# x also given with its columns on partitions: the opening loads, multiplies and waits of an encoder block rearranged

## What is computed

```python
n = rms_norm(h, norm1_g[l])
p = n @ w_in[l]                       # (256 x 1024) @ (1024 x 1536)
qa, ka, va, qb, kb, vb = jnp.split(p, splits, axis=-1)
...
ob = mixer_window(qb, kb, vb, sink[l], rel_bias)   # scores + rel_bias[bucket], then softmax
mix = jnp.concatenate([rms_norm(oa, gnorm_a[l]), rms_norm(ob, gnorm_b[l])], axis=-1)
h = h + mix @ w_o[l]
h = h + hier_moe(rms_norm(h, norm2_g[l]), w_group[l], b_group[l], w_expert[l], b_expert[l],
                 w_gate[l], w_up[l], w_down[l])
```

## Time and profile before

| | us |
|---|---|
| median of 3 runs | 605.11 (604.78 to 606.01) |
| the profiled execution | 604.16 |
| its span in the profile | 602.3 |
| PE busy | 514.4 (85% of the span) |
| DVE, ACT, POOL busy | 132.3, 71.0, 28.2 |
| moved by DMA | 217.56 MB, mean 361 GB/s |

### The profile page before, as it was taken

The page is one execution under the profiler, slowest core; times in us unless marked ns, Lnnn a source line. Parts: engine busy times, 40 slices in busy tenths (PEclk is TensorE's granted clock), DMA queues, the critical chain, the costliest instruction groups (busy, mean ns, idle before and its releaser), DMA issues.

```text
span 602.3 us, 6699 instructions
## 1 busy us (share of the span) xinstructions
PE 514.4 (85%) x2681; PEld 240.9 (40%) x2681; DVE 132.3 (22%) x308; ACT 71.0 (12%) x140; POOL 28.2 (5%) x58
## 2 busy tenths in 40 slices
PE   4999799978999999999999999999959553855294
PEld 2445577546444453535353535353514110411031
DVE  1005565334102020303030303030303000300023
ACT  2013324131010101010101000000100000000002
POOL 2032020040000000000000000000000000000001
PEclk9999999986999999999999999999989856986699
DMA  6898491152889999999999999999999999999991
GB/s 251 326 385 365 175 383 13 36 207 108 299 344 432 425 423 430 429 428 429 430 428 429 427 429 430 429 428 427 425 431 427 428 424 431 429 425 429 414 373 72
DMA packets 23944, 217.56 MB, mean 361 GB/s; under 512 B 5041, under 2 KB 6089, under 8 KB 12401
## 3 DMA queue, kind: packets, MB, share of 16 engines
q1 hardware_dynamic: 19680, 214.31, 85.3%
q10 hardware_dynamic: 4240, 2.94, 1.6%
HBM read 216.18 MB, written 1.06 MB: 361 GB/s over the span
## 4 chain that ended last, share of the span: by engine, by line
PE 71%; DMA 22%; SPq 3%; DVE 2%; issue 1%; ACT 0%; POOL 0%; DVEq 0%; POOLq 0%; ACTq 0%
PE bank L1206 27%; PE bank L1221 13%; PE bank L1178 7%; DMA ring<-in_w_down_dram 7%; PE bank L1241 6%; DMA ring<-in_w_gate_dram 5%; DMA ring<-in_w_up_dram 5%; PE bank L1073 5%; PE bank L1004 4%; DMA ring<-bias_line 3%; PE bank L1063 2%; SPq L366 2%; PE bank L1041 1%; PE bank L1052 1%; PE bank L987 1%
## 5 line engine op out<-in xcount | busy, mean ns | idle before, releaser
L1206 PE MATMUL bank<-ring,region_x 128*64 128x512 f32 (+1 forms) x1024 | 191.9, 636 | 50.6 <-DMA ring<-in_w_up_dram 27.6
L1206 PEld LDWEIGHTS bank<-ring,region_x 128*64 128x64 f32 (+1 forms) x1024 | 60.8, 134 | 178.7 <-issue 178.7
L1221 PE MATMUL bank<-ring,region_q 128*64 128x512 f32 (+1 forms) x512 | 95.7, 624 | 7.0 <-DMA ring<-in_w_down_dram 5.7
L874 DVE TENSOR_TENSOR region_q<-region_q,bank 128x512 f32<-128x512 f32 x13 | 8.9, 687 | 312.5 <-PE bank L1206 312.5
L1221 PEld LDWEIGHTS bank<-ring,region_q 128*64 128x64 f32 (+1 forms) x512 | 29.7, 131 | 63.8 <-issue 61.4
L1178 PE MATMUL bank<-region_q,region_t 128*128 128x128 f32 x416 | 51.1, 284 | 1.8 <-DVE region_q L861 1.8
L1241 PE MATMUL bank<-region_x,region_q 128*128 128x512 f32 x104 | 50.6, 618 | 0.7 <-ACT region_x L606 0.7
L1178 PEld LDWEIGHTS bank<-region_q,region_t 128*128 128x128 f32 x416 | 50.1, 200 | 1.8 <-issue 1.8
L1004 PE MATMUL bank<-ring,region_x 128*128 128x512 f32 x96 | 42.6, 596 | 2.2 <-DMA ring<-in_w_in_dram 1.4
L880 DVE TENSOR_TENSOR h<-h,bank 128x512 f32<-128x512 f32 x52 | 35.7, 687 | 21.9 <-PE bank L1241 21.9
L606 ACT ACTIVATE region_x<-bank 128x512 f32<-128x512 f32 x26 | 15.5, 597 | 135.0 <-PE bank L1221 135.0
(11 more groups left out here) (172 smaller groups left out, 248.5 us busy)
## 6 DMA issues: line engine op xcount, KB each, us to landing
ring<-in_w_gate_dram SPq DMA_DIRECT2D x32, 2048.0 KB, 18.4
ring<-in_w_up_dram SPq DMA_DIRECT2D x31, 2048.0 KB, 16.1
ring<-in_w_down_dram SPq DMA_DIRECT2D x27, 2048.0 KB, 18.1
ring<-in_w_down_dram SPq DMA_DIRECT2D x20, 512.0 KB, 13.8
ring<-in_w_in_dram SPq DMA_DIRECT2D x8, 768.0 KB, 9.4
ring<-in_w_o_dram SPq DMA_DIRECT2D x2, 2048.0 KB, 8.6
ring<-in_w_up_dram SPq DMA_DIRECT2D x4, 512.0 KB, 5.6
ring<-bias_line ACTq DMA_DIRECT2D x1, 1536.0 KB, 15.4
```

Of the source, the lines that this page charges most:

```text
L874: dve.tensor_tensor(act_sb, silu_sb, ps[UP][:], ALU.mult).then_inc(act_done, 1)
L1206: last = pe.matmul(ps[bank][rows, :], xgT[:, c, rows], slots[fill_slot(f + a)][:, c * F:(c + 1) * F], start=(c == 0), stop=(c == KC - 1))
L1221: last = pe.matmul(ps[GD0 + half][rows, :], hT[:, c, rows], slots[fill_slot(f + a)][:, c * D + 512 * half:c * D + 512 * half + 512], start ...
```

## The change

The host hands over two more tensors: `x_cols`, x with its columns on partitions (1 MB, in the layout of `xT`), and `gain_cols`, the norm weights in the layout of `gT`. The rows of x are loaded too, for the squares' sums and the residual.

- SP loads `gT`, then `xT` in four pieces (256 KB each) alternating with the first four chunks of `w_in`; after the sixth chunk come the rows of x, then the last two chunks, then `cst`. Only then does SP wait, for `bias_in`, ahead of `w_o` and the first experts. The waits inside `w_in` are gone.
- The transposes of the norm weights and of x on PE are gone, and their copies on DVE. DVE multiplies `xT` in place, one chunk of 128 x 256 at a time.
- PE waits for each chunk of `xT` by itself.
- DVE sets 128 x 640 numbers to zero, and PE multiplies zeros with zeros: two products with 512 columns ahead of line 979's product, and two behind it. Nothing reads their results.
- ACT issues the bias load ahead of the squares' sums, and only when the sixth chunk of `w_in` has landed.
- PE's wait for `cst` moves from ahead of the first transpose to ahead of the first transpose of the attention.

```diff
--- before.py
+++ after.py
@@ -196,6 +195,7 @@
+        zeros = region_t[:, 0:640]
...
@@ -297,19 +298,16 @@
 
         @block.sync
         def _(sp):
+            sp.dma_start(gT[:], gain_cols).then_inc(gain_in, 16)
+            for c in range(KC):
+                if c < 4:
+                    sp.dma_start(xT[:, 2 * c:2 * c + 2, :], x_cols[:, 2 * c:2 * c + 2, :]).then_inc(xT_in[c], 16)
+                sp.dma_start(w_in_sb[:, c, :], w_in_c[c]).then_inc(w_in_in[c], 16)
+                if c == 5:
+                    for t, arrived in enumerate((x_in, x1_in)):
+                        sp.dma_start(h[:, t, :], x_t[t]).then_inc(arrived, 16)
             sp.dma_start(cst[:], consts).then_inc(consts_in, 16)
-            for t, arrived in enumerate((x_in, x1_in)):
-                sp.dma_start(h[:, t, :], x_t[t]).then_inc(arrived, 16)
-            sp.dma_start(gain_rows[0:8, :], norm1_g.rearrange("l (c p) -> (l c) p", p=P)).then_inc(gain_in, 16)
-            sp.dma_start(gain_rows[8:12, :], gnorm_a.rearrange("l (c p) -> (l c) p", p=P)).then_inc(gain_in, 16)
-            sp.dma_start(gain_rows[12:16, :], gnorm_b.rearrange("l (c p) -> (l c) p", p=P)).then_inc(gain_in, 16)
-            sp.dma_start(gain_rows[16:24, :], norm2_g.rearrange("l (c p) -> (l c) p", p=P)).then_inc(gain_in, 16)
-            for c in range(KC):
-                if c == 3:
-                    sp.wait_ge(line_stored, 16)
-                if c == 7:
-                    sp.wait_ge(bias_in, 16)
-                sp.dma_start(w_in_sb[:, c, :], w_in_c[c]).then_inc(w_in_in[c], 16)
+            sp.wait_ge(bias_in, 16)
             sp.dma_start(w_o_sb[:, 4:8, :], w_o_c[:, 4:8, :]).then_inc(slot_in[4], 16)
...
@@ -476,17 +473,17 @@
 
             act.wait_ge(line_ready, 1)
             act.activation(line_sb, ps[7][0:8, :], ACT.Copy).then_inc(line_cut, 1)
-            act.wait_ge(x_in, 16)
-            act.activation(junk, h[:, 0, :], ACT.Square, accum_out=ssx[:, 0:1]).then_inc(ssx_ready, 1)
             act.wait_ge(line_masked, 1)
             act.dma_start(bias_line, line_sb).then_inc(line_stored, 16)
-            act.wait_ge(x1_in, 16)
-            act.wait_ge(ssx_ready, 1)
-            act.activation(junk, h[:, 1, :], ACT.Square, accum_out=ssx[:, 1:2]).then_inc(ssx_ready, 1)
             act.wait_ge(line_stored, 16)
+            act.wait_ge(w_in_in[5], 16)
             shifted = bass.AP(bias_line.tensor, 0, [[1, P], [4 * P, 8], [1, 3 * P]])
             act.dma_start(bias_sb, shifted).then_inc(bias_in, 16)
-
+            for t, arrived in enumerate((x_in, x1_in)):
+                act.wait_ge(arrived, 16)
+                if t:
+                    act.wait_ge(ssx_ready, 1)
+                act.activation(junk, h[:, t, :], ACT.Square, accum_out=ssx[:, t:t + 1]).then_inc(ssx_ready, 1)
 
             act.wait_ge(rstd1_ready, 1)
@@ -639,14 +636,12 @@
                 ins.then_inc(dve_chain, 1)
                 dve.wait_ge(dve_chain, n[0])
 
-            dve.wait_ge(gains_turned, 1)
-            link(dve.tensor_copy(gT[:], ps[6][:, 0:24]))
-            for t in range(TT):
-                for b in range(2):
-                    dve.wait_ge(x_turned, 2 * t + b + 1)
-                    dve.tensor_tensor(xT[:, 4 * b:4 * b + 4, t * P:(t + 1) * P],
-                                      ps[(4 if t == 0 else 6) + b][:].rearrange("p (c t) -> p c t", c=4),
-                                      bcast(gT[:, 4 * b:4 * b + 4], 2, P), ALU.mult).then_inc(xT_ready, 1)
+            dve.memset(zeros, 0.0).then_inc(zeros_ready, 1)
+            dve.wait_ge(gain_in, 16)
+            for c in range(KC):
+                if c % 2 == 0:
+                    dve.wait_ge(xT_in[c // 2], 16)
+                dve.tensor_scalar(xT[:, c, :], xT[:, c, :], gT[:, c:c + 1], None, ALU.mult).then_inc(xT_ready, 1)
 
             dve.wait_ge(k_squared, 1)
@@ -975,26 +970,21 @@
 
         @block.tensor
         def _(pe):
+            def multiply_zeros(n):
+                for _ in range(n):
+                    pe.matmul(ps[6][:], zeros[:, 0:P], zeros[:, P:P + 512], start=True, stop=True)
+
+            pe.wait_ge(zeros_ready, 1)
+            multiply_zeros(2)
             pe.wait_ge(onehot_in, 32)
             pe.matmul(ps[7][0:8, :], relb_sb, onehot_sb, start=True, stop=True).then_inc(line_ready, 1)
-            pe.wait_ge(consts_in, 16)
-            pe.wait_ge(gain_in, 16 * 4)
-            pe.transpose(ps[6][:, 0:24], gain_rows[0:24, :], ident[0:24, 0:24]).then_inc(gains_turned, 1)
+            multiply_zeros(2)
 
             def turn(dst, srcs, done):
 
                 for k, src in enumerate(srcs):
                     last = pe.transpose(dst[:, k * P:k * P + src.shape[0]], src, ident[0:src.shape[0], 0:src.shape[0]])
                 last.then_inc(done, 1)
-
-            pe.wait_ge(x_in, 16)
-            for b in range(2):
-                turn(ps[4 + b], [h[:, 0, c * P:(c + 1) * P] for c in range(4 * b, 4 * b + 4)], x_turned)
-            pe.wait_ge(x1_in, 16)
-            pe.wait_ge(line_cut, 1)
-            pe.wait_ge(xT_ready, 1)
-            for b in range(2):
-                turn(ps[6 + b], [h[:, 1, c * P:(c + 1) * P] for c in range(4 * b, 4 * b + 4)], x_turned)
...
@@ -1004,8 +994,8 @@
                 return pe.matmul(ps[bank][:], xT[:, c, t * P:(t + 1) * P], cols, start=(c == 0), stop=(c == KC - 1))
 
 
-            pe.wait_ge(xT_ready, 4)
             for c in range(KC):
+                pe.wait_ge(xT_ready, c + 1)
                 pe.wait_ge(w_in_in[c], 16)
                 qkv(0, KV, c, 0)
                 qkv(1, KV, c, 1)
@@ -1076,6 +1066,7 @@
                 return last
 
 
+            pe.wait_ge(consts_in, 16)
             pe.wait_ge(qkv_cut, 3)
             turn(ps[4], [pair_cols(0, b) for b in range(5, 9)], qk_turned)
@@ -1343,7 +1334,10 @@
     nc = _bacc.Bacc("TRN2", target_bir_lowering=False, num_devices=1)
     arrays, args = {}, []
     consts, onehot = shape_constants()
-    every = [(n, inputs[n]) for n in _INS] + [("consts", consts), ("onehot", onehot)]
+    x_cols = inputs["x"][0].reshape(S, KC, P).transpose(2, 1, 0)
+    gain_cols = _np.concatenate([inputs[n][0].reshape(-1, P).T for n in ("norm1_g", "gnorm_a", "gnorm_b", "norm2_g")], 1)
+    every = [("x", inputs["x"]), ("x_cols", x_cols), ("gain_cols", gain_cols)]
+    every += [(n, inputs[n]) for n in _INS[1:]] + [("consts", consts), ("onehot", onehot)]
```

9 lines of the change are left out of this document (4 added, 5 removed).

## The result

The changed kernel takes 599.39 us (median of 4 runs, 597.57 to 600.06), the kernel before 605.56 on the same occasions. The ratio is 0.9891 with a 95% interval of 0.9853 to 0.9929. The forecast was 598.9 out of 605.11. By the profiled executions alone the forecast was 604.16 - 6.3 = 597.9; the changed kernel's took 600.02 us, which is 4.1 less than before.

The account below looks back on a forecast made before the run. The end was taken as fixed by when TensorE lets the unbroken stream of loads begin, near 180 us, and its bytes. 604.16 - 6.3 = 597.9; the median lies 0.95 above: 598.8, rounded to 598.9; range 596.2 to 602.2.

Parts of the forecast that it names:

- A gain of the opening reaches the end one for one: Opening to end: TensorE earlier by some time starts the unbroken loads, near 180 us, and the end earlier by as much.
- G = 15.8 - S, capped by the loads: Projection block: its end comes 6.3 us earlier; w_in's eighth chunk, landing at 26.7, caps the gain near 7.1.
- S: Start of the first projection pass on TensorE: 14.10 us before, 9.5 forecast, between 7.9 and 10.4 by the clock.
- G: Time by which the projection block, and with it the end, comes earlier: 6.3 us, forecast range 4.8 to 7.1.
- The case with all of the bias ahead: Opening's loads: all 1.57 MB of bias ahead of w_in's eighth chunk, at rate 0.375, lands it at 31.5; gain 2.3.
- the bound of the loads: Opening: w_in's eighth chunk lands at 26.7 us, 0.8 ahead of TensorE's need, so loads are nearly a second bound.
- Zeros hidden, clock up in time: Opening on TensorE: first two zero products hidden ahead of the one-hot product; full pace comes between 5.4 and 9.9 us.
- That zeros would not raise the clock: Rival, opening: six slow passes, projection starts at 10.4 and slow; gain 3.2 us, time 601.9; chance 0.08.
- The price that the prediction put on them: Opening on TensorE: one-hot and zeros as six passes on the path, 2.6 us at 2.4 GHz to 5.0 at 1.2.
- The transposes of before: Opening of the kernel before: transposes from 9.56 us warmed TensorE, so zeros win nothing that the transposes didn't give.
- What moves off the path: Square sums, constants and bias come later at no cost: covers 6 us, 1.6 us (POOL's rotary operations) and 11 us.
- Later, 0 +- 1.5 us: Router, low clock from 132.40 to 146 us: its place against the work may shift the time +-1.5 us, middle 0.

Follow-up runs that it names:

- run 1: The changed kernel once more, nothing edited, against the kernel before: 599.95 us, ratio 0.9886.
- run 8: The changed kernel with ACT's five small loads issued behind the store of the bias's line, against the kernel before: 596.00 us, ratio 0.9853.
- Run 4: The changed kernel without ACT's wait for the sixth chunk of w_in ahead of the bias load, against the kernel before: 601.71 us, ratio 0.9911.
- run 10: The changed kernel with clock-holding products (two in the attention, six and two in the router) and ACT's small loads late, against the kernel before: 593.44 us, ratio 0.9800.
- run 6: The changed kernel with clock-holding products in the router's waits, five and one, against the kernel before: 595.43 us, ratio 0.9836.
- run 7: The changed kernel with clock-holding products, two in the attention and five and one in the router, against the kernel before: 593.97 us, ratio 0.9818.
- run 11: The changed kernel with x by rows behind w_in, small loads late, clock-holding products (two in attention, six and two in router), against the kernel before: 593.96 us, ratio 0.9803.
- run 3: The kernel before with only the waits inside w_in's loads removed, against the kernel before: 605.32 us, ratio 0.9971.
- run 12: The kernel before, opening untouched, with clock-holding products (two in the attention, six and two in the router), against the kernel before: 600.05 us, ratio 0.9896.

## Why the prediction was right

- **A gain of the opening reaches the end one for one.** Right. Fourteen profiles have 453.2 to 455.0 us from the first expert to the end.
- **G = 15.8 - S, capped by the loads.** The form was right; both sizes were off, and in opposite ways. S was 8.70 and not 9.5, and by run 1 what set it was the first chunk's landing, at 8.6 and not 6.2 (the zeros' end fell on the same moment in the first profile and 0.3 ahead of it in run 1). The reckoning took 0.39 MB per us from 4 us on, where its own rows have 255 GB/s up to 8 us, and 1.2 MB ahead of the chunk; by 8.6 us DMA had moved about 1.7 MB in the changed kernel (an estimate from 234 GB/s over 6 us, 403 over 0.6 and some 0.02 before), so by this estimate bytes of loads behind it went ahead of its last ones. Small loads are a part of it (run 8: 7.7). The eighth chunk landed at 27.4 and not 26.7, and TensorE waited ahead of the seventh. By the formula with the measured S, G would be 7.1. The 0.9 between went to the wait of 0.30, the second tail of 0.27, and 0.35 in the first 36 passes, which took 16.05 and not 36 x 0.429 + 0.27 = 15.71, as the second and third chunk's began late. So two errors in S and in the loads met, and 6.2 came out near 6.3 by luck in part. The case with all of the bias ahead was summed wrongly: (10.1 - 0.46) / 0.375 + 4.7 is 30.4 us and not 31.5, and G is then 3.4 and not 2.3. Run 4, which comes near that case, has 43.53 - 41.72 = 1.8, of which slow passes took 1.7. Run 4 shows the bound of the loads, runs 8 and 10 that an earlier start runs into it.
- **Zeros hidden, clock up in time.** In the first profile the second set ran at full pace. That zeros would not raise the clock is refuted: in seven of the ten profiles with zeros the clock list's first full stretch begins at 4.6 to 6.3 us, when only zeros and the one-hot product had run, and without them nowhere before 12.5. But in runs 6, 7 and 11, with the same zeros, it begins at 10.2 to 13.3, outside the 5.4 to 9.9 that the prediction gave; the six passes were slow or nearly all, and the projection started at 10.4 to 10.9, the S of that rival. Without the zeros the time is the same within 0.3%. The price that the prediction put on them, 6 x 0.43 to 6 x 0.84 us on the path, was partly none: the first chunk wasn't there before 8.6.
- **The transposes of before.** I said that they had warmed TensorE as zeros do. Runs 3 and 12 have both ways: in run 3 the 64 passes took 27.73, at full pace from the first; in run 12, with the same transposes, 29.53. The first full stretch begins at 12.92 before and at 13.37 in run 3, while the transposes ran, and at 17.84 in run 12, 3.65 us into the projection. So they did in some executions and not in others, and the statement was too strong. That transposes bring no full clock, as the Trainium skill's page "TensorE: Matmul & The Clock Gate" has it in Part 4, isn't borne out by run 3 and the kernel before.
- **What moves off the path.** The bias landed at 31.8 and had 10.9 us of cover (11 reckoned); POOL was done with `rstd1` at 25.5, 5.0 ahead of ACT's first cut (6 reckoned). `cst` came at 29.1 instead of 28, and POOL's cover was 0.5 and not 1.6 us. It held.
- **Later, 0 +- 1.5 us.** The place was wrong. I looked at the router, where the low clock takes 13.7 us before and after, and missed the attention, where it takes 0, 3.4, 6.8 or 10.2 us. The first profile lost 2.8 us there and run 1 won 1.4, against before. This is a larger spread than the term allowed.

The 6.2 us of the opening and the 6.2 us between the medians are the same number partly by chance: a median of four runs with such a spread is no better than its interval, 4.3 to 8.9 us, and the profiled pair differs by 4.1. That the gain is real is shown by run 1, which has 0.9886 with six runs more.

**What stays open.** The interval of no run here is narrow enough to price the zeros or the order of x's loads in time. Why DMA moves only 283 GB/s between 2 and 8 us even without the small loads wasn't tried. How the start's gain divides between the transposes, the loads' order and the zeros isn't shown, and nothing here tells in which executions the clock rises or falls: the first profile and run 6 have TensorE's first six passes at the same times within 0.01 us, and the first full stretch begins at 6.25 in one and at 10.76 in the other.

## What to carry to other kernels

When TensorE and a load both wait at the head of a kernel, reckon them as two bounds and take the later one for each chunk; an earlier start runs into the next chunk's landing. Where TensorE waits for a chain of another engine, look whether the stages behind it run at half clock: products that nothing reads, fitted into three such waits here, brought 1.0% by themselves (run 12), with no change of the data's way.

## What was not expected of the hardware

- The granted clock in the attention was 0.50 for 10.2 us in one execution of the changed kernel and 1.00 in the same window of another. Where it was low it stayed low although TensorE was busy for 9.16 of the 10.20 us, with products of 65 columns and transposes.
- Two waits of 3.07 and 2.86 us for loads, both at the projection, were each followed by 3.4 us at 0.50, which began 1.2 and 1.3 us after the wait had ended, with TensorE busy again.
- In the router 1.08 and 0.59 us of idle ahead of a stage went with a gather at 5.44 us; with 0.23 and none it took 3.73.
- Products of zeros went ahead of a full clock from 4.6 to 6.3 us in seven executions and from 10.2 to 13.3 in three.
- DMA moved 234 GB/s from 2 to 8 us, with 14 loads issued by 4 us and more behind them, and 403 from 8 to 10.
